# Nine norms with tokens on partitions, hand-over by chunk, first tiles side by side, and products of zeros between stages

## What is computed

```python
def rms_norm(x, gain):                       # rms_norm_2 reads the same
    y = x * rsqrt(mean(x * x, axis=-1) + 1e-6)
    return y * gain
def modulate(h, shift, scale): return h * (1 + scale) + shift

# first block
h = swiglu(rms_norm(x, ffn1_pre), ...);  x = x + 0.5 * rms_norm(h, ffn1_post)
u = rms_norm(x, mix_pre)
... three attention branches, gates ...
x = x + rms_norm(merged @ w_out, mix_post)
h = swiglu(rms_norm(x, ffn2_pre), ...);  x = x + 0.5 * rms_norm(h, ffn2_post)
# second block
for l in range(2):
    mod = silu(c) @ w_ada[l] + b_ada[l]      # sh1, sc1, g1, sh2, sc2, g2
    proj = modulate(rms_norm_2(x, mixer_norm[l]), sh1, sc1) @ w_in[l]
    ... conv and pool branches, gates ...
    x = x + g1 * (mixed @ w_out[l])
    h2 = modulate(rms_norm_2(x, ffn_norm[l]), sh2, sc2)
    x = x + g2 * experts(h2)                 # router: 4 groups of 8, top 2
return rms_norm_2(x, final_norm)
```

## Time and profile before

| | |
|---|---|
| device time, three runs | 1904.72, 1903.43, 1903.24 us (median 1903.43) |
| the profiled execution's own time | 1904.18 us |
| its span | 1902.5 us |
| mean granted TensorE clock over the span | 0.953 |
| busy: TensorE, its weight load | 1755.5 us, 1606.4 us |
| busy: VectorE, ScalarE, GpSimd | 1439.0, 1033.2, 3.7 us |
| DMA | 420.85 MB, mean 221 GB/s |

### The profile page before, as it was taken

One profiled execution on the slowest core, in us unless ns is written; L12 is line 12 of the kernel. 1 busy time (PEld: TensorE's weight loads), 2 busy tenths in 40 slices (PEclk: granted clock), 3 DMA queues, 4 the chain that ended last, 5 costly groups with the idle time before them and its releaser, 6 DMA issues.

```text
span 1902.5 us, 32318 instructions
## 1 busy us (share of the span) xinstructions
PE 1755.5 (92%) x11664; PEld 1606.4 (84%) x11668; DVE 1439.0 (76%) x2067; ACT 1033.2 (54%) x1421; POOL 3.7 (0%) x9
## 2 busy tenths in 40 slices
PE   7999999899899799988996999999799969999997
PEld 7899999899889699978896788888698957888886
DVE  7788876733547688888975688888789767888886
ACT  4444464224545434343152788888632437888884
POOL 0000000000000000000000000000000000000000
PEclk9999998997999899998996999999999979999998
DMA  8888643114224498862351699998724517989893
GB/s 341 324 316 305 216 158 123 64 62 160 100 101 166 145 350 309 304 239 89 132 176 59 213 329 331 322 338 318 269 100 133 199 38 246 332 317 338 318 335 131
DMA packets 115510, 420.85 MB, mean 221 GB/s; under 512 B 12784, under 2 KB 12800, under 8 KB 115152
## 3 DMA queue, kind: packets, MB, share of 16 engines
q1 hardware_dynamic: 114336, 414.12, 61.0%
q0 software_dynamic: 1072, 5.31, 0.7%
HBM read 416.76 MB, written 2.62 MB: 220 GB/s over the span
## 4 chain that ended last, share of the span: by engine, by line
PE 65%; DVE 20%; ACT 6%; issue 5%; DMA 4%; DVEq 0%; ACTq 0%; SPq 0%
PE work L741 24%; PE acc L741 10%; PE work L1323 7%; DVE wlo L1796 5%; DVE yconv L2307 5%; PE work L811 4%; DMA raw<-wstream_d 4%; ACT whi L1383 3%; PE work L1335 3%; PE work L719 2%; PE work L1269 2%; PE acc L1362 2%; PE work L752 1%; DVE hf L1817 1%; PE work L796 1%
## 5 line engine op out<-in xcount | busy, mean ns | idle before, releaser
L1796 DVE TENSOR_TENSOR wlo<-raw,whi 128x1024 fp32r<-128x1024 f32 x648 | 778.1, 1223 | 276.4 <-ACT whi L1383 273.1
L1383 ACT ACTIVATE whi<-raw 128x1024 fp32r<-128x1024 f32 x648 | 675.1, 1056 | 403.3 <-PE work L741 257.6
L741 PE MATMUL work<-hhi,whi 128*128 128x256 f32 x1024 | 296.0, 289 | 28.9 <-DVE hlo L1812 24.7
L741 PE MATMUL work<-hlo,whi 128*128 128x256 f32 x1024 | 294.3, 287 | 0.0
L741 PE MATMUL work<-hhi,wlo 128*128 128x256 f32 x1024 | 294.1, 287 | 0.0
L741 PEld LDWEIGHTS work<-hhi,whi 128*128 128x128 f32 x1024 | 199.6, 195 | 32.0 <-issue 30.4
L741 PEld LDWEIGHTS work<-hlo,whi 128*128 128x128 f32 x1024 | 200.0, 195 | 0.0
L741 PEld LDWEIGHTS work<-hhi,wlo 128*128 128x128 f32 x1024 | 199.8, 195 | 0.0
L1895 DVE SCALAR_TENSOR_TENSOR ada_tiles<-ada_tiles,c_act 128x1024 f32<-128x1024 f32 x96 | 116.4, 1219 | 0.0
L752 PE MATMUL work<-hf,raw 128*128 128x256 f32 x512 | 111.5, 379 | 0.0
L752 PEld LDWEIGHTS work<-hf,raw 128*128 128x128 f32 x512 | 97.1, 190 | 13.1
(11 more groups left out here) (416 smaller groups left out, 3520.3 us busy)
## 6 DMA issues: line engine op xcount, KB each, us to landing
raw<-wstream_d SPq DMA_DIRECT2D x688, 512.0 KB, 4.7
ada_tiles<-ada_d SPq DMA_DIRECT2D x96, 512.0 KB, 5.1
bias_rows_d<-rt POOLq DMA_DIRECT2D x1, 1536.0 KB, 7.9
consts<-consts_d POOLq DMA_DIRECT2D x1, 1063.0 KB, 8.1
xT<-x_d SPq DMA_DIRECT2D x4, 256.0 KB, 4.1
mem_in<-mem_d POOLq DMA_DIRECT2D x1, 1024.0 KB, 5.4
tb<-bias_rows_d POOLq DMA_DIRECT2D x1, 1024.0 KB, 7.1
out_d<-hf SPq DMA_DIRECT2D x4, 256.0 KB, 2.5
```

What stands on the lines that cost most here:

```text
L741: mm = pe.matmul(out, a, b, start=(start and k == 0), stop=(stop and k == n - 1), skip_group_check=skip)
L1383: act.activation(whi[n % AHEAD][:], raw[SPLITS[n] % RAW][:], ACT.Copy).then_inc(s("hi_done"), 1)
L1796: dve.tensor_tensor(wlo[n % AHEAD][:], raw[SPLITS[n] % RAW][:], whi[n % AHEAD][:].bitcast(F32), ALU.subtract).then_inc(s("lo_done"), 1)
```

## The change

**Nine norms turned** (0, 4, 5, 6, 7, 9, 10, 12, 13; the others stay and are called wide). The squares are now the weights, 128 tokens at a time, and one column of the ones is the moving operand, so that the sum of a token stands on that token's partition: 16 matmuls of one column in the program, 32 executed (`norm_part`, L751). ScalarE takes the root straight from PSUM, 128 x 2, with the mean as scale and epsilon as bias (L1509). VectorE takes the reciprocal of 128 x 2 (L1937). TensorE spreads the two columns to a row on all partitions by two matmuls with the column, repeated, as weights and the identity as moving operand (`norm_row`, L773). VectorE's scaling reads that row from PSUM; in norms 4 and 6 it is copied to SBUF first. The step that made mean plus epsilon goes.

**Hand-over by chunk.** `hf_done`, `h_high` and `h_ready` count single chunks. In the modulated norms VectorE only scales, and ScalarE adds the shift (Identity with a bias column, L1528) and then takes the high part (L1522).

**First tiles.** FFN 1 begins with two tiles in halves of four chunks (`halved_tiles`), FFN 2 and both mixers of the second block with three tiles side by side, chunk by chunk (`first_tiles`). One turn of FFN 2's loop is written out.

**Zeros.** `hold(bank, n)` multiplies zeros, bf16, 128 x 512, into `work[1]` n times (L761), in TensorE's queue between the parts of the sums, behind the spreading products and ahead of what follows: 105 in all (8, 11, 7, 11, 14, 22, 10 and 22 for norms 0, 4, 5, 6, 7, 9, 10 and 12, none at the last norm).

**The rest.** One root of a single number (`root_table`, L1515) ahead of the last squares of each stage loads the root's table. The last weight tile's high part and rest are moved behind the norm's root or scaling, at the end of FFN 1, FFN 2 and all three `wout`. At the start SyncE loads the identity and 64 columns of the parameters, three weight tiles, c, one more tile, and then the other parameters; GpSimd's queue loads the other constants.

```diff
-PEELED = {"ffn1": 2, "ffn2": 0}
+PEELED = {"ffn1": 2, "ffn2": 1}
+WIDE = (1, 2, 3, 8, 11)
+NORM_BANK = {k: 3 if k in (0, 5, 7, 10) else 0 for k in NARROW}
...
-                sp.dma_start(params[:, 0:NFIRST], ...)
+                sp.dma_start(consts[:, 0:P], ...)
+                sp.dma_start(params[:, 0:8 * DC], ...)
...
+            def norm_part(k, j):
+                pe.wait_ge(s("norm_sq"), NORM_AT[k] + j + 1)
+                for m in (2 * j, 2 * j + 1):
+                    for q in range(QT):
+                        mm = pe.matmul(work[bank][:, q:q + 1], hf[:, m, q * P:(q + 1) * P], ones[:, 0:1], ...)
...
+            def hold(bank, n):
+                if bank in reader:
+                    pe.wait_ge(s(reader[bank][0]), after(*reader[bank]))
+                for _ in range(n):
+                    pe.matmul(work[bank][:, :], zero[:, :], spread(zero[:, 0:1], (512,), (0,)), start=True, stop=True)
+            def norm_sum(k, before=(0, 0, 0, 0)):
+                for j in range(4):
+                    hold(1, before[j])
+                    norm_part(k, j)
+            def norm_row(k, hold_after):
+                pe.wait_ge(s("norm_rstd"), ROWS[k])
+                for q in range(QT):
+                    mm = pe.matmul(work[NORM_BANK[k]][:, q * P:(q + 1) * P], spread(roots_of[:, 2 + q:3 + q], (P,), (0,)),
+                                   ident, start=True, stop=True)
+                mm.then_inc(s("norm_row"), 1)
+                hold(1, hold_after)
...
+            def first_tiles(r, banks, part):
+                tiles = [tile_ready(r + n) for n in range(len(banks))]
+                for c in range(DC):
+                    pe.wait_ge(s("h_ready"), DC * H_INDEX[part] + c + 1)
+                    for bank, (h, l) in zip(banks, tiles):
+                        mm = product(work[bank][:, 0:T], ...)
...
-            norm_sum(0, 0)
-            pe.wait_ge(s("params_loaded"), 16)
+            hold(1, 8)
+            norm_sum(0)
+            pe.wait_ge(s("ident_loaded"), 16)
+            norm_row(0, 0)
...
-            out_tiles("wout", "merged_ready", 0, 4)
-            norm_sum(5, 0)
+            out_tiles("wout", "merged_ready", 0, 4, 0, 11)
+            norm_sum(5, (0, 2, 2, 2))
+            norm_row(5, 1)
             swiglu("ffn2", "x_ready", 4 * 3)
-            norm_sum(6, 0)
+            norm_sum(6)
+            norm_row(6, 11)
...
-                norm_sum(k, 0)
+                norm_sum(k, (0, 2, 2, 2) if l == 0 else (2, 0, 0, 0))
+                norm_row(k, 8)
...
-                out_tiles(f"wout{l}", "mixed_ready", 4 * l, k + 2)
+                out_tiles(f"wout{l}", "mixed_ready", 4 * l, k + 2, 5, 17)
...
+            def shifted(part, l, at):
+                for c in range(DC):
+                    act.wait_ge(s("scaled"), DC * MODULATED[part] + c + 1)
+                    act.activation(hf[:, c, :], hf[:, c, :], ACT.Identity, bias=mod[...]).then_inc(s("hf_done"), 1)
+                    if part in H_INDEX:
+                        high_h(part, (c,))
...
+            root_table()
             squares_ffn(1, START["a0"])
             roots(6)
+            hi(NUMBER[START["a0"] - 1] + AHEAD)
...
+            def rstd_row(k):
+                dve.wait_ge(s("norm_std"), k + 1)
+                dve.reciprocal(roots_of[:, 2:4], roots_of[:, 0:2]).then_inc(s("norm_rstd"), 1)
+                dve.wait_ge(s("norm_row"), ROWS[k])
+                row_of[0] = work[NORM_BANK[k]][:, 0:T]
+                if k in (4, 6):
+                    own(dve.tensor_copy(rstd[:], row_of[0]))
+                    row_of[0] = rstd[:]
...
+            def modulated(part, src, scale):
+                for c in range(DC + 2):
+                    if c < DC:
+                        scaled_chunk(c, src, scale).then_inc(s("scaled"), 1)
+                    if part in H_INDEX and c > 1:
+                        rest_chunk(part, c - 2)
```

More of the change, by code:

```diff
@@ L625, in load_ada @@
                 sp.dma_start(ada_tiles[:, a % ADA_RING, :], src).then_inc(s(f"ada_loaded{a % ADA_RING}"), 16)
-            load(0)
-            load(1)
+            for r in range(3):
+                load(r)
             sp.dma_start(c_act[:], c_d).then_inc(s("c_loaded"), 16)
-            for r in range(2, RAW):
+            load(3)
+            sp.dma_start(params[:, 8 * DC:NFIRST], params_d[:, 8 * DC:NFIRST]).then_inc(s("params_loaded"), 16)
+            for r in range(4, RAW):
                 load(r)
@@ L756, in feature_tile @@
                 for c in range(DC):
-                    if part and c % 2 == 0:
-                        pe.wait_ge(s("h_ready"), 4 * H_INDEX[part] + c // 2 + 1)
                     a = slice(c * P, (c + 1) * P)
@@ L919, in _ @@
                                            + [("dv", m) for m in range(4)]):
-                feature_tile(START[stage] + m, hhi, hlo, n % 4, part="mix" if n == 0 else None)
+                feature_tile(START[stage] + m, hhi, hlo, n % 4)
             def scores(g):
@@ L1716, in _ @@
                 roots(k + 2)
+                hi(NUMBER[START[f"wout{l}"] + DC - 1] + AHEAD)
+                shifted(f"experts{l}", l, 3)
                 act.wait_ge(s("router_centred"), 2 * l + 1)
@@ L1812, in rest_pair, with rest_chunk, scaled_chunk @@
+            def rest_chunk(part, c):
+                dve.wait_ge(s("h_high"), DC * H_INDEX[part] + c + 1)
                 dve.tensor_tensor(hlo[:, c, :], hf[:, c, :], hhi[:, c, :].bitcast(F32), ALU.subtract
                                   ).then_inc(s("h_ready"), 1)
+            def scaled_chunk(m, src, gain):
+                return dve.scalar_tensor_tensor(hf[:, m, :], src(m), gain(m), row_of[0], ALU.mult, ALU.mult)
             def scaled_pair(j, src, gain):
-                for m in (2 * j, 2 * j + 1):
-                    ins = dve.scalar_tensor_tensor(hf[:, m, :], src(m), gain(m), rstd[:], ALU.mult, ALU.mult)
@@ L1830, in normalise @@
                     if between:
-                        between(j)
-                    if j > 0:
-                        rest_pair(part, j - 1)
-            def modulated(part, src, scale, shift):
-                own(scaled_pair(0, src, scale))
-                for j in range(4):
-                    shifted_pair(j, shift)
-                    if j < 3:
-                        ins = scaled_pair(j + 1, src, scale)
-                    if part in H_INDEX and j > 0:
-                        rest_pair(part, j - 1)
-                    if j < 3:
-                        own(ins)
-                if part in H_INDEX:
-                    rest_pair(part, 3)
+                        between(c)
@@ L2290, in _ @@
                 k = 7 + 3 * l
-                variance(k, D)
-                root_done(k)
-                modulated(f"mixer{l}", x_chunk, lambda m: gs_col(l, 0, m), lambda m: mod_col(l, 0, m))
+                rstd_row(k)
+                modulated(f"mixer{l}", x_chunk, lambda m: gs_col(l, 0, m))
                 if l == 0:
```

204 lines of the change are left out of this document (135 added, 69 removed).

## The result

The changed kernel took 1895.41 us in the median of 17 runs (1890.97 to 1902.44). The kernel before, run 17 times beside it, took 1907.76 (1902.22 to 1912.20). The ratio is 0.9946 with a 95% interval of 0.9934 to 0.9958, so it is faster by 0.54%, 8 to 13 us (the two medians lie 12.3 us apart). Forecast were 25 us and 1878.4, with a range of 1869 to 1893: the direction was right, the size was over twice too large, and the time lies outside the range.

A forecast was written before the change was run, and what follows sets the result against it. TensorE, busy 92% of the span, was taken as the bound, with its waits and half clock between stages. Eight places' gains summed to 25.0 us off 1904.18, and 0.75 for the median gave 1878.4 us; range 1869 to 1893.

The forecast's parts named there:

- (5): Into the first layer's experts: shorter root, earlier router start and router products nearer full clock; 6.0 us gained.
- (7): Into the second layer's experts: shorter root, earlier router start and router products nearer full clock; 6.0 us gained.
- The last norm's 1.9: End of the kernel: root 1.5 us, sum 0.2, row not copied; 1.9 us gained with hand-overs (1.5 to 2.1).
- term (4): FFN 2 to the first mixer: earlier sum, two shorter roots, faster hand-over, less lost clock; 5.8 us gained (3 to 7.3).
- (3): Before FFN 2: norms win 4.3 us, but three tiles side by side leave TensorE idle, then half clock; 0.3 us gained.
- rival C: A later engine takes part of the gain back, at the mixers too; 12.5 us left, 1890.9 us; chance 0.10.
- Term (6): Into the second mixer: root 1.5 us, sum 0.2, hand-over 2.3, less 1.0 of clock; 3.0 us gained (0 to 4.1).
- Term (1): Start of the kernel: root saves 1.5 us, sum up to 0.9, two tiles by halves limit it; 1.0 us gained.
- Term (2): End of FFN 1: squares no longer wait behind the last tile copy, but a weight rest comes later; 1.0 us gained.
- A: The clock is held everywhere, one-column sums included; 33.0 us gained, 1870.4 us; chance 0.17.
- B: The clock is not held: one-column sums pull it down, zeros run at half rate; 10.4 us gained, 1893.0 us; chance 0.20.
- D: Slower: unfinished zeros stand on the path when squares or chunks arrive; 1916 us with half of them there; chance 0.03.

The follow-up runs named there:

- run 17: Not a follow-up run: words of "run 17 times", the kernel before, unaltered, measured 17 times beside the changed kernel: median 1907.76 us.
- e7: The kernel before with 30 zero products ahead of each router, nothing else changed: 1901.11 us, ratio 0.9967.
- e5: The changed kernel, but both mixers of the second block begin with two tiles side by side, not three: 1886.87 us, ratio 0.9895.
- e6: The changed kernel, but both mixers of the second block begin with one tile, by single chunks: 1888.56 us, ratio 0.9902.
- e4: The changed kernel, but FFN 2 begins with one tile, not three side by side: 1891.90 us, ratio 0.9927.
- e12: e9 with FFN 1 too beginning with one tile, no zeros ahead of the first norm, and norm 0 as before the change: 1884.10 us, ratio 0.9876.
- e2: The changed kernel without its 105 zero products, all else kept: 1910.51 us, ratio 1.0022.
- e9: The changed kernel with the edits of e4 and e5 together: 1883.02 us, ratio 0.9874.

## Why the prediction was wrong

**The single operations were right.** A root of 0.27 us (0.3), a reciprocal of 0.17 (0.17), spreading in 0.7 at full and 1.2 at half clock, one-column products at 0.11 or 0.22, zeros at 0.22 or 0.43. Terms (5) and (7), the experts, were forecast at 6.0 each and came at 5.4 and 6.9. The router was better than forecast, 3.8 against 4.7 us. The last norm's 1.9 lies between the 1.1 and 3.5 measured. Three other steps failed.

**First, the price of the turned norms.** The forecast took 1.5 us for each root, near the upper end of its 1.0 to 1.6, and let the sums gain besides. From the end of the last square to the first scaling the nine norms together won 6.0 us (41.5 to 35.5). Norms 4, 7, 9 and 12 won 1.5 to 1.7 each, the rest between 0.9 won and 0.9 lost. Two things were mis-sized: the spreading ran at half clock in six norms, and the one-column sums at half clock outlasted the wide ones.

**Second, in term (4): "The gain lasts, since VectorE's convolution runs without a gap from that product on".** Up to the first GLU product the term was right, though the table's row hides it: that row begins within FFN 2 and holds 1.7 us lost behind the first down product, which belongs to (3). From FFN 2's last product to the GLU product it is 35.65 us before and 30.46 in the changed kernel, 5.2 gained where 5.8 was forecast. The base is uncertain here too: e7, which has the code of before up to there, took 38.7. The last down products of before, then of e7 with its GLU product; the lines of the changed kernel stand further up:

```profile
840.76 3.10 PE acc L741 x24
```

```profile
843.88 3.11 PE acc L741 x24
...
885.71 0.44 DVE vpad L2326
```

The convolution did run without a gap. But TensorE, now ahead of it, waited for it at the layer norm, fell to half clock and gave 2.6 to 2.8 us back. This is rival C's mechanism (a later engine takes part of it back), at a place that it did not name, and e5 and e6 show it. C had a chance of 0.10, which was too low.

**Term (6)** took 3.0 us for the second mixer; 1.2 came up to the GLU product, and 1.5 went at the second layer norm. The cause is the same. With two tiles (e5) or one (e6) the place wins 2.9 and 3.0 us.

**Third, term (3).** Its mechanism was right: the fifth tile's copy late, 8.1 us of VectorE's row, 5.7 us of idle time (5.8 measured) and the half clock behind it. From the first product of FFN 2 to the input of the first down product 13.2 us became 17.3, 4.1 lost, near the 3.9 that follow from 8.6 against 4.71. What failed is the 4.3 us that the two norms were to win against it. The second sum was to run "nearer full clock" and win 1.0; it took 7.5 us in place of 5.7, since from 650 us on the clock stood at 0.50, parts and zeros alike. TensorE also clears `acc` between the row and the first tile, 1.7 us, which before lay in a gap. So 0.3 gained was forecast, with 2.5 lost as the bound, and 2.1 to 3.6 were lost up to the down product's input, and 1.5 to 1.7 behind it. The chain of the changed kernel there:

```profile
650.51 1.50 PE work L751 x8
652.01 0.88 PE work L761 x2
652.89 1.51 PE work L751 x8
...
656.59 1.71 PE acc L922 x4
658.29 8.24 PE work L791 x66
```

**Term (1)** took 1.0 us gained; 2.6 to 3.6 were lost with this start at half clock, 0.6 to 0.8 where it began at full clock (e4 to e6). The sum was priced as if it ran near full clock. In the changed kernel all 32 one-column products ran at half, and they outlast 16 wide ones that wait for the last square anyway. A further 1.5 us goes between the first down product and the bias rows in the changed kernel and in e4 to e6 alike, with a fall of the clock at 31 to 40 us that every kernel with the change has. It stayed when the two tiles, the start's zeros and the narrow norm 0 were all gone (e12), so it comes with another part of the change (the order of the loads, the hand-over by chunk); which one was not tried.

**Term (2)**, 1.0, is right in six of the nine kernels of the table that have the change (0.7 to 1.0). The changed kernel's own profile, e5 and e6 lost 0.4 to 0.5 instead, and in all three the stretch at half clock near 260 us was the longer one.

**Rivals A, B and D.** The zeros' worth was underrated in kind: A had said that they hold the clock, and against the kernel without them they are worth 15 us. But they do so from a worse ground. In e2 what was booked as thirteen or so us of shorter roots is nothing: the nine norms save 8.5 us behind their sums and lose 8.3 in them. B's sum, 10.4 us, is near the measured difference, by luck: its parts are not the measured ones, since it had the routers win 3.7 each and the start lose nothing. D did not happen, though the zeros stand on the chain as it said.

**The base.** The forecast subtracted from an execution that was fast by some 3.5 us in the first mixer. From the later median, 25 us less is 1882.8, and the range, moved by the same 4.3 us, would have ended at 1897.3 and just held the result. The forecast gain would still have been twice the measured one.

## What to carry to other kernels

When an engine is made faster ahead of a chain that another engine owns, look for where the two meet again: the lead comes back there as a wait, and a wait costs twice if a clock falls in it. Start a stage with just as many tiles as the next engine needs for its first step, here one or two instead of three; that was worth as much again as the whole change (1883.0 us in e9 against 1895.4). Price a clock by running the kernel without what is to hold it, and compare executions place by place, since whole times of one kernel differ by 10 us here, while the places of the second block up to its second router repeat within 0.3. Check the base in the same way: e7 shows two places of the kernel before that differ by 3 us between two profiles of the same code.

## What the runs showed of the hardware that was not expected

- Thirty zero products right ahead of a router, or 17 behind the norm's row, put all of its 32 products of 36 columns at full clock, 3.76 us against 7.04. In every kernel with the change that had them the first router's place gained 5.3 to 5.5 us and the second's 6.7 to 7.4, against 1.6 and 3.0 in e2.
- The Trainium skill (TensorE: Matmul & The Clock Gate, "Part 1: The HAM clock gate") tells of a gate that follows how busy the array has been. The routers agree with it: 7.04 us behind a gap, 3.76 behind zeros. The fall at 306.3 us in the earlier trace rows, which the prediction held against it, is weaker than it looked: TensorE had stood still for 1.57 us until 305.34. The changed kernel has a better case. Two stretches of it (columns as in the earlier trace rows):

```profile
856.20:859.70 3.50, 3.49 (x33) 3.40 (x31) 2.51 (x5) 0.71 (x2) 0.00 (x0) 1.00 0.45 152
861.40:863.80 2.40, 2.40 (x8) 0.79 (x6) 2.28 (x6) 0.00 (x0) 0.00 (x0) 0.52 0.00 0
```

In the first it does one-column products without a pause, behind full-width ones; after 0.5 us without work and the spreading the zeros of the second begin at half clock. So the clock fell behind products that had kept the engine busy, and no run here settles why.
- At the start the same code reaches full clock by 5.5 us in some executions and only at 16 us or later in others, and the granted clock of the first stretch reads 1.00 in both; only the durations tell (0.43 us a zero product).
